# Exps over two PSUM banks at once, SWAP products in the general banks, and Squares that may run on VectorE

## The reference

```python
a = rms_norm(h, g_attn_pre)
z = a @ w_in                      # FoX q|k|v|forget logit, SWA q|k|v
log_f = log_sigmoid(ff + b_forget)
# FoX: 8 heads of 64, causal, logit[t,s] += sum over s<j<=t of log_f[j]
# SWA: 8 query heads, 2 key/value heads, window 128, T5 bias, a sink per head
h = h + rms_norm(concat(fox, swa) @ w_out, g_attn_post)
m = rms_norm(h, g_ff_pre)
h = h + rms_norm(square(relu(m @ w_ff1)) @ w_ff2, g_ff_post)
gate = sigmoid(h @ w_ple_gate)
h = h + rms_norm((p @ w_ple) * gate, g_ple_post)
```

## Time and profile before

| | us |
|---|---|
| median of two runs | 1145.02 (1139.12 and 1150.92) |
| the profiled execution | 1138.93 |
| its span, slowest core (core 4) | 1137.2 |
| its cores | 1134.1 to 1137.2 |
| TensorE, VectorE, ScalarE busy | 981.6, 566.2, 449.2 |
| mean granted clock of TensorE | 0.963 to 0.966 |

### The profile page before, as it was taken

How to read it: one execution, slowest core, us unless ns; L and a number is a source line. 1 busy time by engine, 2 the same in 40 slices (tenths; PEclk the granted TensorE clock), 3 DMA queues, 4 the chain that set the end, 5 groups by cost and what they waited for, 6 DMA issues and landing times.

```text
span 1137.2 us, 21286 instructions; the slowest of 8 cores (1134.1 to 1137.2 us)
## 1 busy us (share of the span) xinstructions
PE 981.6 (86%) x5049; PEld 447.7 (39%) x5142; DVE 566.2 (50%) x879; ACT 449.2 (40%) x823; POOL 74.3 (7%) x79
## 2 busy tenths in 40 slices
PE   2269878889999988996999999987999999997872
PEld 0025444535454533342444444432444444433331
DVE  4287668662333311577766402318666404136765
ACT  3245555578878778465100001123000101035443
POOL 1020000000000000000000111110000111100000
PEclk9999999999999988996999999997999999998996
DMA  9826233200202150014356699992556899980223
GB/s 221 195 23 50 22 30 30 37 5 3 39 4 38 54 134 1 2 18 58 49 78 77 78 147 145 144 149 28 75 75 75 97 146 144 142 122 1 75 75 148
DMA packets 119354, 86.23 MB, mean 76 GB/s; under 512 B 21384, under 2 KB 109704, under 8 KB 118456
## 3 DMA queue, kind: packets, MB, share of 16 engines
q0 software_dynamic: 109232, 61.35, 45.2%
q1 hardware_dynamic: 10000, 23.52, 6.5%
HBM read 137.72 MB, written 8.49 MB: 129 GB/s over the span
## 4 chain that ended last, share of the span: by engine, by line
PE 71%; DVE 13%; issue 7%; ACT 4%; SPq 3%; DMA 2%; DVEq 0%; ACTq 0%
PE ps L388 71%; DVE X L406 4%; DVE hT L406 4%; SPq L450 3%; DVE ZO L406 3%; ACT RS L397 2%; DMA X<-maskS 2%; DVE RE L406 1%; DVE RO L406 1%; DVE RS L406 1%; ACT L397 1%; ACT DT L397 0%; ACT SQ L397 0%; ACT ZO L397 0%; ACT PT L397 0%
## 5 line engine op out<-in xcount | busy, mean ns | idle before, releaser
L388 PE MATMUL ps<-X,WS 128*128 128x512 bf16 x1594 | 386.7, 385 | 21.0 <-DVE X L406 11.0
L388 PE MATMUL ps<-ZO,WS 128*128 128x512 bf16 x1379 | 318.5, 380 | 1.5
L388 PEld LDWEIGHTS ps<-X,WS 128*128 128x128 bf16 x1632 | 159.1, 99 | 212.9 <-issue 48.3
L397 ACT ACTIVATE PT<-ps 128x512 bf16<-128x512 f32 (+3 forms) x382 | 185.7, 548 | 46.4 <-PE ps L388 40.7
L388 PEld LDWEIGHTS ps<-ZO,WS 128*128 128x128 bf16 x1408 | 138.0, 98 | 161.7 <-issue 2.4
L397 ACT ACTIVATE SQ<-ps 128x512 bf16<-128x512 f32 x64 | 37.9, 597 | 288.4 <-PE ps L388 155.2
L406 DVE COPY X<-ps 128x512 f32<-128x512 f32 x40 | 27.7, 691 | 190.7 <-PE ps L388 190.7
L388 PE MATMUL ps<-SQ,ONESB 128*128 128x512 bf16 x159 | 71.4, 462 | 55.8 <-ACT SQ L397 49.4
L435 POOL DMA_DIRECT2D WS<-w_ff x48 | 50.6, 1054 | 647.4 <-PE ps L388 647.4
L388 PE MATMUL ps<-PT,ZO 128*128 128x512 bf16 (+3 forms) x216 | 65.8, 340 | 10.3 <-DVE ZO L406 7.3
L388 PE MATMUL ps<-ZO 128*128 128x256 bf16 (+6 forms) x221 | 68.4, 339 | 1.5 <-ACT PT L397 0.3
(11 more groups left out here) (71 smaller groups left out, 739.3 us busy)
## 6 DMA issues: line engine op xcount, KB each, us to landing
WS<-w_ff POOLq DMA_DIRECT2D x48, 1024.0 KB, 12.0
hT<-xT SPq DMA_DIRECT2D x4, 2048.0 KB, 25.7
yT<-hT SPq DMA_DIRECT2D x3, 2048.0 KB, 6.9
hT<-xT SPq DMA_DIRECT2D x4, 1024.0 KB, 11.9
WS<-w_in POOLq DMA_DIRECT2D x13, 256.0 KB, 8.2
WS<-w_out POOLq DMA_DIRECT2D x2, 1024.0 KB, 11.1
WS<-w_gate POOLq DMA_DIRECT2D x2, 1024.0 KB, 12.1
yT<-hT SPq DMA_DIRECT2D x8, 256.0 KB, 2.3
```

Of the source, the lines that this page charges most:

```text
L388: return pr.add("pe", lambda e: e.matmul(out, lhsT, rhs, start=start, stop=stop, skip_group_check=True), reads, writes, cost=c)
L397: return lambda e: e.activation(out, in_, func, **kw)
```

## The change

- `schedule` adds `ACT_PEN`, 300 ns, to ScalarE's estimated finish where an operation may go to either engine. It affects the choice of engine, not the times that follow.
- The first four PSUM banks become two tensors of two banks (`PSa`, `PSb`); `PSP[i]` views one as 128x2x512. The accumulators move from banks 3 and 4 to 4 and 5 (`ACCA`, `ACCB`).
- `PT` becomes two tiles of 128x2x512 (`PTP`) where there were three of 128x512.
- Sliding window: both key tiles of a query tile get their scores in the two banks of a pair, and one exp covers both. FoX: both heads of a key tile likewise; P times V follows one pair behind.
- The SWAP product no longer has bank 5 but takes the next general bank, 6 or 7, in both attentions.
- `stats_add` has `sbsrc`: where the source lies in SBUF (the prenorms, phase 7) the Square becomes an `anyop`, on ScalarE or as a product on VectorE.

```diff
@@ schedule
+        ACT_PEN = 300.0
...
                 for (e, c, a) in opts:
                     st = max(rt[i], free[e])
-                    if best is None or st + c < best[0] + best[2]:
+                    v = st + c + (ACT_PEN if (len(opts) > 1 and e == "act") else 0.0)
+                    if best is None or v < bestv:
                         best = (st, e, c, a)
+                        bestv = v
@@ build_program
-        NPT = 3
+        NPT = 2
-        PT = [sb("PT%d" % i, [128, 512], BF16) for i in range(NPT)]
+        PTP = [sb("PT%d" % i, [128, 2, 512], BF16) for i in range(NPT)]
-        PS = [stack.enter_context(nc.psum_tensor("ps%d" % i, [128, 512], F32)) for i in range(8)]
+        PSa = stack.enter_context(nc.psum_tensor("psa", [128, 1024], F32))
+        PSb = stack.enter_context(nc.psum_tensor("psb", [128, 1024], F32))
+        PS = [PSa[:, 0:512], PSa[:, 512:1024], PSb[:, 0:512], PSb[:, 512:1024]]
+        PS += [stack.enter_context(nc.psum_tensor("ps%d" % i, [128, 512], F32))[:, :] for i in range(4, 8)]
+        PSP = [PSa[:, :].rearrange("p (a x) -> p a x", a=2), PSb[:, :].rearrange("p (a x) -> p a x", a=2)]
+        ACCA, ACCB = 4, 5
@@ stats_add
-            act(SQ[i][:, :], src, AF.Square, src_reads, [("sq", i)])
+            if sbsrc:
+                anyop(src_reads, [("sq", i)], SQ[i][:, :], (SQ[i][:, :], src, AF.Square), "tensor_tensor",
+                      (SQ[i][:, :], src, src, ALU.mult))
+            else:
+                act(SQ[i][:, :], src, AF.Square, src_reads, [("sq", i)])
@@ sliding window
-                        act(PT[pti][:, :], PS[sbk][:, :], AF.Exp, [("ps", sbk)], [("pt", pti)])
-                        pts.append((pti, kb))
-                    for ii, (pti, kb) in enumerate(pts):
-                        mm(PS[3][:, jn * 256:(jn + 1) * 256], VS[:, kb, 0:128], PT[pti][:, 0:256],
+                        pts.append((ti, kb))
+                    nt = len(tiles)
+                    act(PTP[pti][:, 0:nt, :], PSP[pi][:, 0:nt, :], AF.Exp,
+                        [("ps", 2 * pi + ti) for ti in range(nt)], [("pt", pti)])
+                    for ii, (ti, kb) in enumerate(pts):
+                        mm(PS[ACCA][:, jn * 256:(jn + 1) * 256], VS[:, kb, 0:128], PTP[pti][:, ti, 0:256],
...
-                mm(PS[5][:, :], SWAP[:, :], DEN[di][:, :], True, True,
-                   [("den", di, a, c) for a in range(2) for c in range(2)] + [("c", "swap")], [("ps", 5)])
-                act(RC[di][:, :], PS[5][:, :], AF.Ln, [("ps", 5)], [("rc", di)])
+                swb = genbank()
+                mm(PS[swb][:, :], SWAP[:, :], DEN[di][:, :], True, True,
+                   [("den", di, a, c) for a in range(2) for c in range(2)] + [("c", "swap")], [("ps", swb)])
+                act(RC[di][:, :], PS[swb][:, :], AF.Ln, [("ps", swb)], [("rc", di)])
@@ FoX (the SWAP product as above)
+                pend = []
+                for j in range(nj):
...
+                    pi = sp_i[0] % 2
...
+                    for hd in (0, 1):
+                        sbk = 2 * pi + hd
...
+                    act(PTP[pti][:, :, 0:N], PSP[pi][:, :, 0:N], AF.Exp, [("ps", 2 * pi), ("ps", 2 * pi + 1)],
+                        [("pt", pti)])
+                    pend.append((j, pti, c0, N))
+                    if len(pend) > 1:
                         emit_PV(pend.pop(0))
@@ phase 7
-                stats_add(mixt[:, mc, :], [(mkey, mc)], msb, mc == 0, mc == 7)
+                stats_add(mixt[:, mc, :], [(mkey, mc)], msb, mc == 0, mc == 7, sbsrc=True)
```

More of the change, by code:

```diff
@@ L478, in build_program, with stats_add @@
         rs_i = [0]
-        def stats_add(src, src_reads, msb, first, last):
+        def stats_add(src, src_reads, msb, first, last, sbsrc=False):
             i = sqtile()
-            act(SQ[i][:, :], src, AF.Square, src_reads, [("sq", i)])
+            if sbsrc:
[3 more added lines that the diff above has]
+                act(SQ[i][:, :], src, AF.Square, src_reads, [("sq", i)])
             mm(PS[msb][:, :], ONESB[:, :], SQ[i][:, :], first, last, [("sq", i), ("c", "ones")], [("ps", msb)])
@@ L581, in build_program @@
         s_i = [0]
+        sp_i = [0]
         pt_i = [0]
@@ L645, in build_program @@
                     tiles = ([0] if n > 0 else []) + [1]
+                    pi = sp_i[0] % 2
+                    sp_i[0] += 1
+                    pti = pt_i[0] % NPT
+                    pt_i[0] += 1
                     pts = []
-                    for tl in tiles:
+                    for ti, tl in enumerate(tiles):
                         kb = n - 1 if tl == 0 else n
[L649 to L652, removed]
+                        sbk = 2 * pi + ti
                         mm(PS[sbk][:, :], IDB[:, :], BMv[:, tl, g, :], True, False, [("c", "id"), ("c", "bm")],
@@ L750, in build_program, with emit_PV @@
                 nj = 4 * tg + 4
-                items = [(hd, j) for j in range(nj) for hd in (0, 1)]
-                def emit_S(hd, j, tg=tg):
+                def emit_PV(st, nj=nj):
+                    j, pti, c0, N = st
+                    mm(PS[ACCA][:, c0:512], VF[:, j, 0:128], PTP[pti][:, 0, 0:N], j == 0, j == nj - 1,
+                       [("pt", pti), ("VF", j // 4, 0), ("VF", "ones")], [("ps", ACCA)])
+                    mm(PS[ACCB][:, c0:512], VF[:, j, 64:192], PTP[pti][:, 1, 0:N], j == 0, j == nj - 1,
+                       [("pt", pti), ("VF", j // 4, 1), ("VF", "ones")], [("ps", ACCB)])
+                pend = []
+                for j in range(nj):
                     r = j - 4 * tg
@@ L756, in emit_S @@
                     N = 512 - c0
-                    sbk = sbanks[s_i[0] % 3]
-                    s_i[0] += 1
+                    pi = sp_i[0] % 2
+                    sp_i[0] += 1
                     pti = pt_i[0] % NPT
                     pt_i[0] += 1
[L761 to L787, removed]
+                    for hd in (0, 1):
+                        sbk = 2 * pi + hd
+                        if hd == 0:
+                            qt, kt, K = qE, kE, 96
+                            rk = [("qE", tg), ("qE", "aug"), ("kE", j // 4), ("kE", "aug")]
+                        else:
+                            qt, kt, K = qO, kO, 128
+                            rk = [("qO", tg), ("qO", "aug"), ("kO", j // 4), ("kO", "aug")]
+                        mm(PS[sbk][:, 0:N], kt[0:K, j * 128:(j + 1) * 128], qt[0:K, tg * 512 + c0:(tg + 1) * 512],
+                           True, r < 0, rk, [("ps", sbk)])
+                        if r >= 0:
+                            mm(PS[sbk][:, 0:128], IDB[:, :], MFB[:, :], False, True, [("c", "id"), ("c", "mf")],
+                               [("ps", sbk)])
@@ L798, in build_program @@
-                mm(PS[5][:, :], SWAP[:, :], DEN[di][:, :], True, True,
-                   [("den", di, a, c) for a in range(2) for c in range(2)] + [("c", "swap")], [("ps", 5)])
-                act(RC[di][:, :], PS[5][:, :], AF.Ln, [("ps", 5)], [("rc", di)])
+                anyop([("ps", ACCA)], [("den", di, 1, 0), ("den", di, 1, 1)], DEN[di][64:128, :],
+                      (DEN[di][64:128, :], PS[ACCA][64:128, :], AF.Copy), "tensor_copy",
+                      (DEN[di][64:128, :], PS[ACCA][64:128, :]))
@@ new lines, in build_program @@
+                anyop([("ps", ACCB)], [("den", di, 0, 0), ("den", di, 0, 1)], DEN[di][0:64, :],
+                      (DEN[di][0:64, :], PS[ACCB][0:64, :], AF.Copy), "tensor_copy",
+                      (DEN[di][0:64, :], PS[ACCB][0:64, :]))
+                swb = genbank()
+                mm(PS[swb][:, :], SWAP[:, :], DEN[di][:, :], True, True,
+                   [("den", di, a, c) for a in range(2) for c in range(2)] + [("c", "swap")], [("ps", swb)])
+                act(RC[di][:, :], PS[swb][:, :], AF.Ln, [("ps", swb)], [("rc", di)])
@@ L806, in build_program @@
+                dve("tensor_tensor", [("ps", ACCB), ("rc", di)], [("OT", p, tg, 1)],
+                    OT[64:128, p, tg * 512:(tg + 1) * 512], PS[ACCB][64:128, :], RC[di][64:128, :], ALU.mult)
         pr.retire("X2")
```

37 lines of the change are left out of this document (15 added, 22 removed).

## The result

The changed kernel takes 1212.57 us (median) against 1139.08 us of the kernel before in the same comparison, a ratio of 1.0635 with a 95% interval of 1.061 to 1.066: slower, by some 73 us. The forecast was 1195 us, in a range of 1152 to 1237. The profiled execution has spans of 1204.6 to 1211.1 us.

The account below looks back on a forecast made before the run. FoX p=0 to 2 bound by TensorE's own work, the sliding window by a dependence loop through two accumulators; 27 + 24 + 4 + 1 = 56 us on the profiled 1138.9 gives 1195 us, range 1152 to 1237.

Parts of the forecast that it names:

- The term that was named as decisive: Both attentions: SWAP in banks 6 and 7 keeps projections out of tg 0 to 2 and seven of eight sliding-window blocks.
- Sliding window, +27 forecast: Sliding window: blocks of 6.9 us plus projections standing free put the first FoX SWAP at 259 us instead of 232.
- some 2.9 us in every block: Sliding window: TensorE stands still that long from SWAP to the next P times V, and the clock falls.
- My cold end, 7.95 us: Sliding-window block at the 1.2 GHz level: products and SWAP cost about 1.3 us more than in the 6.65 us block.
- FoX, +24 forecast: FoX, p=0 to 2: one period takes 65 us against 57, +8 three times.
- I take 4.5 us as left over: FoX: of 21.4 us of projections per p, 4.5 stay unhidden; bank 7's half lies partly beside the next tg=0.
- Bank 6's half: FoX: the projections given bank 6, 10.7 us of filler, go into tg=3 and the hole at the end of p.
- p=3, +4 forecast: FoX, last three tg of p=3: the slower pair loop makes 52.6 us against 49.
- Squares and ACT_PEN, 0 forecast (-4 to +4): Prenorms, last layer, evacuations: moving work to VectorE costs nothing in sum; the start may save 2 us.
- In the last layer VectorE already leads: Last layer: VectorE is already the leading engine, a ground within the Squares and ACT_PEN term of 0.
- The shared banks cost nothing: Faster rival, both attentions: the scheduler finds other work, blocks and FoX periods get shorter; 1112 us, chance 7%.
- Hardly anything overlaps: Far slower rival, both attentions: projections stand free and TensorE stays at the lower clock; 1262 us, chance 8%.

Follow-up runs that it names:

- e1_swap67_only: The kernel before, with one edit: the SWAP product takes the next general bank, 6 or 7; 1226.18 us, ratio 1.078.
- e4_sq7_on_act: The changed kernel, with the Squares of the last layer (phase 7) on ScalarE alone as before; 1207.41 us, ratio 1.0608.
- e5_pairs_only: e2_swap_in_pair with ACT_PEN at 0 and every Square on ScalarE, leaving the pair exps and their banks; 1142.13 us, ratio 1.0037.
- e7_swa_pairs_fox_single: e5_pairs_only with FoX's exps single again, scores in banks 0 to 2, SWAP in 3; 1133.46 us, ratio 0.995.
- e3_swap_own_bank: The changed kernel, with bank 7 for SWAP and 6 alone for projections from first attention block to end of FoX; ratio 1.039.
- e2_swap_in_pair: The changed kernel, with SWAP in the first bank of the next score pair, banks 6 and 7 for projections alone; 1143.32 us, ratio 1.0053.

## Why the prediction was right, and where its terms were off

**The mechanism held.** The term that was named as decisive, SWAP in the rotation of banks 6 and 7, makes 88 us alone. What was to be seen was seen: no projections in tg 0 to 2, and the first one of the second bank released by the Ln of the SWAP product. The clock was below 0.9 in one of the two sliding-window stretches only (0.92 and 0.88). That the sum came within 18 us has some luck in it: the terms were off by -8 (sliding window), +22 (FoX), -4 (p=3) and +7 us (last layer), in part against each other.

**Sliding window, +27 forecast, +18.8 measured.** Projections standing free: forecast 27.9 and 25.0 us from SWAP to SWAP, measured 31.3 and 26.2; what was added there for the passages (1.6 us for a cold start, 3.5 and 4.5 us to the next SWAP) had no row behind it. The blocks: forecast 6.9 us, measured 41.9 and 43.2 us for seven intervals, 6.1 in the mean. The step that was off is the pause of TensorE, "some 2.9 us in every block", and with it the low clock. The scores follow each exp, and most of them stand behind SWAP, so that the longest pauses in the block shown are 0.83 and 1.05 us, and the granted clock in the two stretches is 0.92 and 0.88. The saving from exps done ahead was larger than my 0.45 us as well: between the multiplies' end and the DEN copies lie 124.07 - 123.94 = 0.13 us where there were 1.64. My cold end, 7.95 us, did come in e1_swap67_only: 7.6 us at a clock of 0.72.

**FoX, +24 forecast, +46.2 measured.** Here the size was off by half. The step is "I take 4.5 us as left over". It had two grounds. Bank 6's half, 10.7 us, was to go into tg=3: only 21 wide ones did, 4.5 us, mostly one between two pair exps. And bank 7's half was to lie beside tg=0 of the next p: hardly any does. Its first scores start at 381.20, its first P times V at 388.77, when most projections are done; the projections stand ahead of the attention in the written order, and tg=0 needs some of them, but which of the two holds it was not tried. So 16.8 of the 21.4 us stand behind tg=3. The other part of the sum was about right: without fillers one p was to take 60.6 us; 72.8 less 16.8 free-standing is 56.0, at a pair pace of 1.15 us instead of 1.19, and ends of tg cheaper than 4.4 us.

**p=3, +4 forecast, 0 measured.** The slower loop was there (1.15 us per pair against 1.02). But 1.02 was read late in tg=3. At its start, behind a pause of 1.91 us, the kernel before had TensorE mostly at the 1.2 GHz level:

```profile
...
432.00:436.00 4.00, 2.31 (x6) 0.45 (x7) 1.38 (x2) 2.04 (x5) 0.00 (x0) 0.58 0.02 4
436.00:440.00 4.00, 3.78 (x11) 1.43 (x12) 0.00 (x0) 2.98 (x6) 0.00 (x0) 0.57 0.00 0
...
```

Its first seven exps there took 439.63 - 434.37 = 5.26 us, 1.50 per pair. The changed kernel has a granted clock of 1.00 from 496 to 505 and its 1.15 us from the first pairs on, and early matmuls of the output projection stand there too (497.33). So what the loop lost in tg=3 the start gave back.

**Output projection +1,** measured 1.6 together with the feed-forward layer.

**Squares and ACT_PEN, 0 forecast (-4 to +4), +7.2 in the last layer.** "In the last layer VectorE already leads" was not so plain, and the conclusion was wrong: before, VectorE was busy 69 of 108 us and TensorE's row, which overstates, 74; in the chain of that stretch VectorE had 33% and TensorE 39%. The scheduler gave VectorE 24 of 32 Squares all the same, 24 x 0.69 = 16.6 us. With them it is the busiest engine, 84 of 115 us, and has 40% of the chain; 7 us came out in the time. With them back on ScalarE (e4_sq7_on_act) the stretch is 108 us again.

**The rivals.** "The shared banks cost nothing" falls with e1_swap67_only. "Hardly anything overlaps" was right for FoX's projections (three quarters of them stand behind tg=3) but not in its condition, a TensorE that stays at the lower level. No run shows a gain from the saved fixed part of the exps: in FoX, where ScalarE is busiest, pairs cost 8 us (227.3 in e5_pairs_only against 219.0 in e7_swa_pairs_fox_single). Before it they gave 9.5 us to the first FoX SWAP (231.6 against 222.1 in e5_pairs_only). The block shown has its exps done ahead, as four exp halves allow where there were three; that this depth is the reason is argued, since no run has pairs without it.

## What to carry to other kernels

Where dependences follow the written order, a buffer that two streams of work share ties them together in that order; a short product put into the filler's rotation takes the filler's freedom away, and a list scheduler can't give it back. Giving that product one of the filler's two banks for itself is no full repair either: the filler then lacks the second. Before an engine is relieved, ask whether a stretch is a chain, a loop or an engine's own work: merged exps came with a shorter sliding-window chain and hurt the FoX loop, and no run shows a gain from the relieved engine's time. A cost penalty in a scheduler moves work by the estimates of one moment, also to an engine that is as busy. And where two versions differ by a few us, compare all cores: the slowest ones alone put the last SWAPs of two kernels 6.0 us apart where the means differ by 2.5.

## What the runs showed that I had not expected

In the changed kernel the pauses of about 1 us in every sliding-window block left the granted clock mostly at the 2.4 GHz level: 0.92 and 0.88 in the two stretches. In e1_swap67_only, with single exps and as little work, it is 0.68 and 0.72. TensorE's pauses there add up to about the same, 16 to 17 us per stretch against 15 to 16, but in each stretch six of them are 1.5 to 1.9 us long, about one per block, where the changed kernel has one above 1.5 and seven between 1.05 and 1.33. Whether this difference between the two loops decides was not tried.

One PSUM bank for projections still carried 45 wide matmuls of them in the three tg behind a period's first SWAP (e3_swap_own_bank), against 57 with two banks (e2_swap_in_pair), though every group has to wait for the evacuation of the one before. In FoX as a whole that still left it 28 us behind two banks (255.6 against 227.4).
